# Two-layer streaming encoder on one core: both attentions reordered, a third slot for split weights, a third output chunk as filler, and the last chunk in token halves

## The chip, the cores and the metric

One core of a Trainium2 chip runs the whole kernel. The metric is device time in microseconds (us) of one execution; the kernel before has a median of 1163.75 us in 3 runs. TensorE (PE) multiplies, VectorE (DVE) and ScalarE (ACT) do the elementwise work, GpSimd (POOL) only constants and a few small powers, SyncE (SP) issues most transfers.

## The reference

The input is one sequence of 512 tokens of width 1024, all in f32. What is computed, cut down:

```python
# layer 0
h = rms_norm(x, norm_mix[0])
qa, ka, va, ra, ga, qb, kb, vb = split(h @ ab_w_in)        # GLA heads | stick-breaking heads
o_a = gla_chunk_causal(...); o_a = rms(o_a) * gla_norm * silu(ra)
o_b = stick_breaking(qb, kb, vb)                           # 8 heads of 64
x = x + concat([o_a, o_b]) @ ab_w_out
x = x + conv_ffn(rms_norm(x, norm_ffn[0]))
# layer 1
q, k, v = split(rms_norm(x, norm_mix[1]) @ c_w_qkv)        # 16 query heads, 4 key heads, window 128
x = x + swa_gqa_sinks(q, k, v, sinks, rel_bias) @ c_w_out
x = x + conv_ffn(rms_norm(x, norm_ffn[1]))
return rms_norm(x, norm_final)
```

Stick-breaking of one head needs z = q.k, then ln(1 + exp(-|z|)), a sum over later keys, an exp, and the product with v. The FFN is an up projection to 2 x 2816, a causal convolution of width 3, gelu(g) * val, and a down projection.

## The kernel before

The activations stand as features x tokens: `x` is 8 chunks of 128 features x 512 tokens. Every large product is made of three f32r matmuls (`three`, L1160 to L1162): an operand is split into a rounded high part and the rest, and hi.hi, hi.lo and lo.hi are summed in PSUM. So each weight unit of 128 x 1024 goes through these steps: a transfer into one of four `w_raw` buffers (SP), `hi` (ACT, L601, rounds it into `w_hi`), `lo` (DVE, L840, the rest into `w_lo`), then 24 matmuls of 512 columns. There are two slots of `w_hi`/`w_lo`, so unit u can be split only when unit u-2 is done.

Each engine runs its own program in order; semaphores join them. In the two mixers one list of steps, `SEQ0` and `SEQ1`, is built by hand and every engine walks it, taking its own part of each step. A weight unit is cut in eighths ("parts") so that attention steps can stand between them. The names in the lists:

- `("unit", u, (a, b))`: parts a to b of unit u on PE. When a unit ends, DVE evacuates it if it is a feature x token tile (L900, L903, L1080, L1083), and ACT if it belongs to a group that is token x feature (`vb`, `va`, `kg`, `v`; `b_evac`, L638, four tiles). Behind the unit stands `split`: `hi` and `lo` of a later unit.
- Layer 0, head h: `z` (PE L1311, L1314; ACT takes the absolute value), `z_exp` and `z_ln` (ACT L660, L663, 128 x 1280), `z_soft` (DVE: `sbS` L924, `sbH` L926, `sbL` L928), `sfx` (PE L1324 needs `sbL`; then ACT L667), `pv` (PE L1333, for two heads). `SB_PARTS` holds how many parts of filler stand between them.
- Layer 0, GLA: `gt`, `gz`, `gs`, `gd`, `gkv`, `go`, `gn`, `gout`, at places by `GLA_AT`, counted in parts. `gkv_v` (DVE L949, L952) makes the states that `go` (PE L1384) reads.
- Layer 1, head pair n: `s` (PE L1430; DVE L1111, L1121, L1124), `s_exp` (ACT L814, L817), `s_norm` (DVE, ends with L1134), `t` (PE transposes L1440, ACT copies L822), `o` (PE L1456; ACT L826, DVE L1139 split it). `v1s` is a copy of `v1` shifted by 64 tokens, made with two transfers issued by ACT (L802, L803) after the evacuation of `v`; every `o` needs it.
- `out`: blocks of an output chunk, which need the split attention output.

After a mixer come its eight output chunks (`w_out`, `out_tiles`), each added to `x` (L861), scaled and split into `h_hi` and `h_lo` (L612, L855) and squared into `ssq`. The 44 up units and 8 x 4 down units of the FFN follow in loops. At the end: the sum of squares over features (`ssq_mm`, L1206), variance (L873), power -0.5 on POOL (L588), a diagonal (L877), a broadcast matmul (`rinv_mm`, L1213), eight scalings of 128 x 512 (L1148) and eight output transfers (L545).

Of the kernel before, what the change touches and what calls it, by code (L numbers as in the profile page):

```python
# [27 lines left out]
F32 = mybir.dt.float32  # L28
# [33 lines left out]
MIX1 = [("k", 0), ("q", 0), ("q", 1), ("k", 1)] + [("q", i) for i in range(2, 7)] + [("v", 0), ("v", 1), ("q", 7)]  # L62
# [49 lines left out]
GLA_AT = ((42, "gt", 0), (45, "gz", 0), (49, "gz_v", 0), (56, "gs", 0), (60, "gd", 0), (62, "gd_v", 0),  # L112
# [120 lines left out]
def trunk(nc, xT, w_mix0, w_mix1, w_up, w_down, small, wg2, bias, out):  # L233
    ctx = ExitStack()
    with ctx:
# [79 lines left out]
        prTs = [s1(f"prT{n}", [P, NCH, P]) for n in range(CH // 2)]  # L315
# [8 lines left out]
        o1_lo = s1("o1_lo", [P, KC, T], F32R)  # L324
        m1.close()
# [268 lines left out]
        def _(act):  # L594
# [107 lines left out]
            def w_out(norm, u0, r0):  # L702

                for c in range(KC):
                    hi_static(u0 + c + SPL)
                    norm_tile(norm, c, r0 + c)

            def ffn(layer, norm, u_up, u_dn, r0, next_cols, last):
# [64 lines left out]

                def down_pair(i, final):

                    for kk in range(1, 9):
                        if not final or kk + SPL < 8:
# [3 lines left out]
                        if kk in (3, 7):  # L781
# [10 lines left out]
            for name, i, span in SEQ1:
                if name == "split":
                    hi_static(U_MIX1 + i + SPL)
                elif name == "unit" and span[1] == 8:
# [38 lines left out]
        def _(dve):  # L834
# [138 lines left out]
            def w_out(norm, u0, r0, units):  # L973
                for c in range(KC):
                    res_add(c, out_bank(c, units), u0 + c + 1)
                    lo_static(u0 + c + SPL)
                    res_split(norm, c, r0 + c)

            def ffn(layer, norm, u_up, u_dn, r0, next_cols, last):
# [74 lines left out]

                def down_pair(i, final):
                    for kk in range(1, 9):
                        j = kk // 4
                        if kk in (3, 7):
                            res_add(j + 2 * i, B_RES + j, u_dn + kk + 1 + 8 * i)
                        if not final or kk + SPL < 8:  # L1060
# [3 lines left out]
                        if kk in (3, 7):  # L1064
# [502 lines left out]
```

## Time and profile before

| | |
|---|---|
| median of 3 runs | 1163.75 us (1162.48 to 1165.25) |
| the profiled execution: its own time | 1162.42 us |
| its span, first to last instruction | 1160.7 us |
| PE busy | 1127.6 us, 97% |
| DVE, ACT busy | 653.8 us, 492.8 us |
| from the span's start to the last large matmul | 1145.07 us |

The rows of the profile name an engine, a line of the kernel and the tiles; "idle before" is the time in which the engine did nothing ahead of the instruction, with what ended it. The stages by the clock of the span: layer 0's mixer to about 235 us, its output and FFN to 640, layer 1's mixer to 755, its output and FFN to 1145, the final norm to the end.

### The profile page before, as it was taken

How to read it: one execution, taken by the hardware profiler on the slowest of the kernel's cores; microseconds unless marked ns; L12 is line 12 of the kernel's file. 1: busy time of each engine (PE TensorE's matmuls, PEld its weight loads, DVE VectorE, ACT ScalarE, POOL GpSimd, SP SyncE). 2: the span in 40 equal slices, each digit the busy share in tenths (PEclk: the TensorE clock that was granted, in tenths of full speed). 3: DMA queues.
4: the chain of work that ended last, by engine and by line, in shares of the span. 5: the costliest groups of instructions: out<-in, count | busy, mean ns of one | idle time of the engine just before them, and what ended most of it. 6: DMA issues, size and time to landing. Idle time of an engine off the chain costs nothing.

```text
span 1160.7 us, 15078 instructions
## 1 busy us (share of the span) xinstructions
PE 1127.6 (97%) x5402; PEld 918.6 (79%) x5402; DVE 653.8 (56%) x837; ACT 492.8 (42%) x714; POOL 8.6 (1%) x25
## 2 busy tenths in 40 slices
PE   8999999999999999999999999899999999999995
PEld 7776777778888888888888777688888888888884
DVE  6324343565777777774333565655777777763333
ACT  5547354843434434443332365634443443432220
POOL 1000000000000000000000000000000000000000
PEclk9999899999999999999999999999999999999997
DMA  5211111122232232223333222132222223233331
GB/s 225 73 55 55 55 55 55 55 91 91 91 107 92 90 106 93 90 77 94 94 99 120 98 73 89 38 104 89 98 90 103 95 90 106 77 85 93 97 86 72
DMA packets 31751, 102.92 MB, mean 89 GB/s; under 512 B 3537, under 2 KB 3682, under 8 KB 31714
## 3 DMA queue, kind: packets, MB, share of 16 engines
q1 hardware_dynamic: 30978, 100.17, 26.2%
q10 hardware_dynamic: 736, 2.24, 0.6%
q8 instruction: 25, 0.41, 0.1%
q14 instruction: 12, 0.10, 0.0%
HBM read 99.84 MB, written 2.10 MB: 88 GB/s over the span
## 4 chain that ended last, share of the span: by engine, by line
PE 59%; issue 32%; ACT 5%; DVE 4%; DMA 1%; POOLq 0%; POOL 0%; ACTq 0%; DVEq 0%; SPq 0%
PE ps L1160 17%; PE ps L1162 17%; PE ps L1161 17%; PE ps L1324 2%; PE ps L1311 2%; ACT pr L817 1%; ACT w_hi L601 1%; PE ps L1333 1%; DVE w_lo L840 1%; DMA x<-xT 1%; PE ps L1456 1%; DVE sc L1111 1%; ACT sbE L663 0%; DVE mx L1121 0%; DVE x L1148 0%
## 5 line engine op out<-in xcount | busy, mean ns | idle before, releaser
L601 ACT ACTIVATE w_hi<-w_raw 128x1024 fp32r<-128x1024 f32 (+1 forms) x203 | 198.1, 976 | 512.9 <-PE ps L1162 512.9
L840 DVE TENSOR_TENSOR w_lo<-w_raw,w_hi 128x1024 fp32r<-128x1024 f32 (+1 forms) x205 | 229.8, 1121 | 243.7 <-ACT w_hi L601 237.8
L1160 PE MATMUL ps<-h_hi,w_hi 128*128 128x512 f32 x896 | 355.6, 397 | 8.2 <-DVE h_lo L855 3.1
L1162 PE MATMUL ps<-h_hi,w_lo 128*128 128x512 f32 x896 | 349.6, 390 | 0.0
L1161 PE MATMUL ps<-h_lo,w_hi 128*128 128x512 f32 x896 | 349.6, 390 | 0.0
L1160 PEld LDWEIGHTS ps<-h_hi,w_hi 128*128 128x128 f32 x896 | 168.6, 188 | 48.1 <-issue 11.6
L1162 PEld LDWEIGHTS ps<-h_hi,w_lo 128*128 128x128 f32 x896 | 168.6, 188 | 35.4
L1161 PEld LDWEIGHTS ps<-h_lo,w_hi 128*128 128x128 f32 x896 | 168.7, 188 | 35.0 <-issue 1.2
L1160 PE MATMUL ps<-y_hi,w_hi 128*128 128x512 f32 x352 | 136.9, 389 | 0.0
L1161 PE MATMUL ps<-y_lo,w_hi 128*128 128x512 f32 x352 | 136.9, 389 | 0.0
L1162 PE MATMUL ps<-y_hi,w_lo 128*128 128x512 f32 x352 | 136.9, 389 | 0.0
L988 DVE TENSOR_TENSOR us<-ps,rinv 128x512 f32<-128x512 f32 x88 | 60.7, 692 | 84.7 <-PE ps L1162 84.7
L1160 PEld LDWEIGHTS ps<-y_hi,w_hi 128*128 128x128 f32 x352 | 66.1, 188 | 13.8
L1162 PEld LDWEIGHTS ps<-y_hi,w_lo 128*128 128x128 f32 x352 | 66.1, 188 | 13.8
L1161 PEld LDWEIGHTS ps<-y_lo,w_hi 128*128 128x128 f32 x352 | 66.1, 188 | 13.5
L998 DVE SCALAR_TENSOR_TENSOR cv<-us,par,cv 128x512 f32<-128x512 f32 x88 | 66.2, 752 | 11.0 <-DVE cv L995 0.6
L725 ACT ACTIVATE cv<-us,par 128x512 f32<-128x512 f32 x88 | 70.6, 804 | 2.9 <-DVE us L988 2.9
L995 DVE SCALAR_TENSOR_TENSOR cv<-us,par,cv 128x512 f32<-128x512 f32 x88 | 65.6, 746 | 0.6 <-ACT cv L725 0.6
L861 DVE TENSOR_TENSOR x<-ps,x 128x512 f32<-128x512 f32 (+1 forms) x32 | 22.1, 691 | 56.2 <-PE ps L1162 56.2
L1160 PE MATMUL ps<-w_hi,h_hi 128*128 128x512 f32 (+2 forms) x128 | 45.3, 354 | 2.7 <-DVE kbT L900 2.6
L1162 PE MATMUL ps<-w_hi,h_lo 128*128 128x512 f32 (+2 forms) x128 | 43.8, 342 | 0.0
L1161 PE MATMUL ps<-w_lo,h_hi 128*128 128x512 f32 (+2 forms) x128 | 43.8, 342 | 0.0
(181 smaller groups left out, 1050.6 us busy)
## 6 DMA issues: line engine op xcount, KB each, us to landing
w_raw<-w_up SPq DMA_DIRECT2D x88, 512.0 KB, 3.2
w_raw<-w_mix SPq DMA_DIRECT2D x53, 512.0 KB, 3.3
w_raw<-w_down SPq DMA_DIRECT2D x32, 384.0 KB, 3.1
w_raw<-w_down SPq DMA_DIRECT2D x32, 320.0 KB, 2.9
out<-x SPq DMA_DIRECT2D x8, 256.0 KB, 2.2
x<-xT SPq DMA_DIRECT2D x2, 512.0 KB, 8.0
x<-xT ACTq DMA_DIRECT2D x2, 512.0 KB, 8.7
bias_sb<-bias ACTq DMA_DIRECT2D x1, 512.0 KB, 3.9
```

The lines of the kernel that those rows point to most:

```text
L601: s.activation(w_hi[r % SPL][:, 0:cols], w_raw[r][:, 0:cols], ACT.Copy).then_inc(w_hi_ready, 1)
L725: s.activation(cv[k % 4][:, :], us[k % 2][:, 2:2 + T], ACT.Identity, bias=par[:, bass.ds(taps + 3, 1)], scale=par[:, bass.ds(taps + 2, 1)] ...
L840: v.tensor_tensor(w_lo[r % SPL][:, 0:cols], w_raw[r][:, 0:cols], w_hi[r % SPL][:, 0:cols].bitcast(F32), ALU.subtract).then_inc(w_lo_ready, 1)
L861: v.tensor_tensor(blk(x, c), ps[:, bank, :], blk(x, c), ALU.add).then_inc(x_updated, 1)
L988: v.tensor_tensor(us[k % 2][:, 2:2 + T], ps[:, k, :], rinv[:, :], ALU.mult).then_inc(u_scaled, 1)
L995: v.scalar_tensor_tensor(cv[k % 4][:, :], us[k % 2][:, 1:1 + T], par[:, bass.ds(taps + 1, 1)], cv[k % 4][:, :], ALU.mult, ALU.add).then_in ...
L998: v.scalar_tensor_tensor(cv[k % 4][:, :], us[k % 2][:, 0:T], par[:, bass.ds(taps, 1)], cv[k % 4][:, :], ALU.mult, ALU.add).then_inc(conv2, 1)
L1160: mm(dst, w[0], m[0], start=first, stop=False, skip_group_check=shared)
L1161: mm(dst, w[0], m[1], start=False, stop=False, skip_group_check=shared)
L1162: return mm(dst, w[1], m[0], start=False, stop=last, skip_group_check=shared)
L1311: mm(zs[:, ZOFF[b]:ZOFF[b] + ZW[b]], kbT[rows, j, b * P:(b + 1) * P], qbT[rows, j, b * P:T], start=b != 3, stop=False, skip_group_check=True)
L1324: ins = mm(dst, lhs[:, :], part[:, ZOFF[c]:ZOFF[c] + ZW[c]], start=False, stop=c == TT - 1 and part is sbL, skip_group_check=True)
```

## The change

1. `b_evac`: the last unit of a group `vb`, `va`, `kg` takes token tiles 1 and 0 first, then 3 and 2; a new semaphore `b_half` lets ACT evacuate two tiles in the middle of the unit and two at its end.
2. `SB_PARTS` and `GLA_AT` get other numbers. From `sfx` of head 1 on, the steps of the heads stand two parts of filler later. The order around the places that matter is listed below.
3. Layer 1: a third slot of `w_hi`/`w_lo` (in memory freed by sharing two of eight `prT` tiles), and each `split` works three units ahead in place of two, through the output chunks too. One more unit is split at the end of layer 0's FFN.
4. Layer 1: the two `v` units come before q6 and q7; `o` 0 to 5 stand earlier; a third output chunk (`out` 2) joins the two that fill PE between the last attention steps.
5. End: the weights of the last output chunk of the last down projection are split into the then free `h_hi`/`h_lo`, all 22 blocks, and used twice, for tokens 0 to 255 and then 256 to 511. The norm of a half, its scalings (128 x 256) and its transfers (256 KB, two chunks each, 1 KB runs) are done by halves; the sum and the broadcast of half 0 stand inside the matmuls of half 1 (before its blocks 5 and 14).

The order of the steps, cut to where it differs (kg1[2:4] is parts 2 and 3 of unit kg1):

```
layer 0, before: z_exp.1 kb1[3:5] z_ln.1 kb1[5:7] z_soft.1 kb1[7:8] split.7 kg0[0:7] sfx.1 kg0[7:8] split.8 kg1[0:2] z.2 pv.0 ...
layer 0, after:  z_exp.1 kb1[3:5] z_ln.1 kb1[5:8] split.7 z_soft.1 kg0 split.8 kg1[0:1] sfx.1 kg1[1:4] z.2 pv.0 ...
before: kg2[0:1] z_ln.2 kg2[1:3] z_soft.2 kg2[3:8] split.10 qb2[0:2] gt qb2[2:3] sfx.2 qb2[3:5] gz qb2[5:8]
after:  kg2[0:3] z_ln.2 kg2[3:5] z_soft.2 kg2[5:8] split.10 qb2[0:2] gt qb2[2:5] gz sfx.2 qb2[5:8]
before: z_exp.3 z_ln.3 kb2[5:7] z_soft.3 kb2[7:8] split.12 gs qb3[0:4] gd qb3[4:6] gd_v qb3[6:7] sfx.3
after:  z_exp.3 kb2[7:8] split.12 gs qb3[0:1] z_ln.3 qb3[1:3] z_soft.3 qb3[3:5] gd qb3[5:7] gd_v qb3[7:8] split.13 va0[0:1] sfx.3
before: z.6 pv.2 qa0[1:6] z_exp.6 z_ln.6 qa0[6:8] split.19 gkv.1 qa1[0:1] z_soft.6 qa1[1:4] gkv_v.1 qa1[4:8] split.20 ra0[0:2] sfx.6 ra0[2:3] go.0
after:  z.6 pv.2 qa0[3:8] split.19 gkv.1 z_exp.6 z_ln.6 qa1[0:3] z_soft.6 qa1[3:4] gkv_v.1 qa1[4:8] split.20 ra0[0:3] go.0 ra0[3:4] sfx.6
before: z_exp.7 ra1[2:3] go.1 go_v.1 ra1[3:4] z_ln.7 ra1[4:6] gn.0 z_soft.7 ra1[6:8] split.22 ra2[0:1] silu.0 ra2[1:3] gn_v.0 ra2[3:4] gn.1 ra2[4:6] sfx.7
after:  go.1 go_v.1 ra1[3:4] z_exp.7 ra1[4:6] gn.0 z_ln.7 ra1[6:8] split.22 z_soft.7 ra2[0:1] silu.0 ra2[1:3] gn_v.0 ra2[3:4] gn.1 ra2[4:8] split.23 sfx.7
layer 1, before: s.5 v0[5:7] t.4 v0[7:8] s_exp.5 v1[0:4] split.9 v1[4:6] s_norm.5 v1[6:8] q7[0:2] t.5 q7[2:4] split.10 o.0 o.1 q7[4:8]
  split.11 o.2 s.6 o.3 s_exp.6 s.7 out0[0,1] out1[0,1] s_norm.6 o.4 o.5 s_exp.7 out0[2,3] t.6 out0[4,5] s_norm.7 o.6 t.7 out1[2,3] o.7 ...
layer 1, after:  s.5 v1[5:7] t.4 v1[7:8] s_exp.5 q6[0:4] split.9 q6[4:6] s_norm.5 q6[6:8] q7[0:2] t.5 o.0 q7[2:4] split.10 o.1 o.2 q7[4:8]
  split.11 o.3 s.6 o.4 o.5 s.7 s_exp.6 out0[0..5] s_norm.6 s_exp.7 out1[0..3] t.6 out1[4,5] s_norm.7 o.6 out2[0,1] t.7 out2[2,3] o.7 ...
```

The diff, cut to its core:

```diff
-SB_PARTS = ((4,), (5, 2, 2, 2, 8), (3, 2, 5, 2, 8), (8, 2, 0, 2, 8), (5, 2, 2, 3, 8), (2, 1, 1, 7, 8),
-            (3, 5, 0, 3, 9), (5, 3, 2, 2, 8), (9,))
+SB_PARTS = ((4,), (5, 2, 2, 3, 9), (3, 2, 5, 2, 8), (8, 2, 2, 2, 6), (5, 2, 2, 3, 8), (2, 1, 1, 7, 8),
+            (3, 5, 0, 3, 9), (5, 3, 2, 2, 8), (7,))
-... (60, "gd", 0), (62, "gd_v", 0),
+... (61, "gd", 0), (63, "gd_v", 0),
+SPL1 = 3
+def slot(u):
+    return (U_MIX1 % 2, (U_MIX1 + 1) % 2, 2)[(u - U_MIX1) % 3] if U_MIX1 <= u < U_UP1 else u % SPL
+def slot_free(u):
+    last = [k for k in range(u) if slot(k) == slot(u)]
+    return max(last[-1] + 1 if last else 0, U_UP0 if slot(u) >= SPL else 0)
+        def out_bank(c, units):
+            if units is MIX1 and c in (2, 3):
+                return B_SC + c - 2
...
+                        if span[0] < 4 <= span[1]:
+                            act.wait_ge(b_half, b_before(MIX0, i + 1) // TT)
+                            b_evac(dst, B_COLS[n], b_tile, order[0:2])
+                        if span[1] == 8:
+                            act.wait_ge(unit_done, i + 1)
+                            b_evac(dst, B_COLS[n], b_tile, order[2:4])
...
-                    hi_static(U_MIX1 + i + SPL)
+                    hi_static(U_MIX1 + i + SPL1)
...
             def w_out(norm, u0, r0, ahead):
                 for c in range(KC):
-                    hi_static(u0 + c + SPL)
+                    if c + ahead < KC + SPL:
+                        hi_static(u0 + c + ahead)
                     norm_tile(norm, c, r0 + c)
...
+            def down_tail(u_dn, r0):
+                ...
+                for half in range(2):
+                    toks = tok_half(half)
+                    for k in range(4):
+                        if half == 0:
+                            pe.wait_ge(w_lo_ready, u_dn + 4 * (KC - 1) + k + 1)
+                        for b in range(DN[k]):
+                            c = DOFF[k] + b
+                            if half == 1 and c == SSQ_AT:
+                                last_sum(0)
+                            if half == 1 and c == RBC_AT:
+                                last_rbc(0)
+                            w = tuple(last_w(t, k)[:, b * P:(b + 1) * P] for t in (h_hi, h_lo))
+                            ins = three(ps[:, B_LAST[half], 0:TH], w, (y_hi[:, c, toks], y_lo[:, c, toks]),
+                                        c == 0, c == FC - 1)
+                    ins.then_inc(half_done, 1)
+                last_sum(1)
+                last_rbc(1)
```

On DVE the end now runs, per half: add, (for half 1: scaling 5 of half 0), `ssq` add, variance, (for half 1: scalings 6 and 7 of half 0), diagonal, then scalings 0 to 4 of half 0 or 0 to 7 of half 1.

## Rows read from the trace of the kernel before

**Rows 1.** Windows: length, busy time of PE, PEld, DVE, ACT, POOL (instructions), then granted clock, DMA, GB/s.

```profile
34.00:235.00 201.00, 192.10 (x1037) 148.94 (x1036) 83.82 (x92) 112.72 (x107) 0.00 (x0) 0.97 0.17 56
660.00:755.00 95.00, 87.80 (x619) 71.50 (x618) 59.18 (x83) 55.66 (x179) 0.00 (x0) 1.00 0.20 67
```

**Rows 2.** Waits of PE in the two mixers: total, times, longest.

```profile
PE ps L1160 <- DVE kbT L900: 2.6, 1, 2.6
PE ps L1360 <- ACT gE L680: 1.8, 1, 1.8
...
PE ps L1160 <- DVE w_lo L840: 3.2, 3, 1.2
PE ps L1456 <- DMA v1s<-v: 1.6, 1, 1.6
```

**Rows 3.** Windows around three waits of PE.

```profile
67.26:69.87 2.61, 0.00 (x0) 0.00 (x0) 2.58 (x4) 0.30 (x1) 0.00 (x0) 0.91 0.00 0
69.87:72.76 2.89, 2.89 (x13) 2.89 (x13) 1.08 (x1) 0.00 (x0) 0.00 (x0) 0.50 0.25 61
...
116.97:120.26 3.29, 3.29 (x16) 3.29 (x17) 3.29 (x4) 0.00 (x0) 0.00 (x0) 0.53 0.00 0
120.26:124.13 3.87, 3.87 (x10) 3.06 (x11) 0.16 (x1) 0.18 (x1) 0.00 (x0) 0.52 0.41 135
718.90:720.50 1.60, 0.00 (x0) 0.02 (x1) 0.96 (x1) 0.61 (x1) 0.00 (x0) 1.00 0.16 51
```

**Rows 4.** ACT in time order, 179 to 184: start, length, instruction.

```profile
179.84 1.28 ACT L663 ACT_TABLE_LOAD   x1
181.13 1.28 ACT L663 ACTIVATE sbE<-sbE 128x1280 f32<-128x1280 f32 x1
183.09 1.06 ACT L601 ACTIVATE w_hi<-w_raw 128x1024 fp32r<-128x1024 f32 x1 [0.68 <-PE ps L1162]
```

**Rows 5.** DVE in time order, 185 to 192.

```profile
185.32 1.48 DVE L924 SCALAR_TENSOR_TENSOR sbS<-ps,sbE 128x1280 f32<-128x1280 f32 x1
...
189.11 0.28 DVE L949 COPY kbT<-ps 128x128 f32<-128x128 f32 x1
189.43 2.65 DVE L952 SCALAR_TENSOR_TENSOR kbT<-kbT,dec,ps 128x128 f32<-128x128 f32 x7
```

**Rows 6.** ACT in time order, layer 1, 709 to 717.

```profile
709.01 0.49 ACT L814 ACTIVATE es<-nm,par 128x4 f32<-128x4 f32 x2 [0.30 <-DVE nm L1124]
712.48 1.05 ACT L601 ACTIVATE w_hi<-w_raw 128x1024 fp32r<-128x1024 f32 x1
714.15 1.57 ACT L638 ACTIVATE v<-ps,rinv_col 128x256 f32<-128x256 f32 x4 [0.62 <-PE ps L1162]
715.75 0.52 ACTq L802 DMA_DIRECT2D v1s<-v  x1
716.30 0.61 ACTq L803 DMA_DIRECT2D v1s<-v  x1
```

**Rows 7.** PE's transposes `t.5`.

```profile
716.41 1.09 PE L1440 MATMUL ps<-ident,pr 128*128 128x128 f32 x8
```

**Rows 8.** DVE as the output chunks end, 784 to 788.

```profile
784.16 0.69 DVE L861 TENSOR_TENSOR x<-ps,x 128x512 f32<-128x512 f32 x1 [1.85 <-PE ps L1162]
785.31 1.23 DVE L840 TENSOR_TENSOR w_lo<-w_raw,w_hi 128x1024 fp32r<-128x1024 f32 x1 [0.46 <-ACT w_hi L601]
786.45 0.75 DVE L855 SCALAR_TENSOR_TENSOR h_lo<-x,par,h_hi 128x512 fp32r<-128x512 f32 x1
```

**Rows 9.** Windows of steady matmuls: 256 columns, 512 columns.

```profile
707.40:713.70 6.30, 6.30 (x55) 6.30 (x54) 1.64 (x4) 5.55 (x20) 0.00 (x0) 1.00 0.03 12
1120.00:1140.00 20.00, 20.00 (x90) 16.57 (x89) 6.51 (x8) 4.44 (x7) 0.00 (x0) 1.00 0.12 33
```

**Rows 10.** The end in time order.

```profile
1150.52 2.08 PE L1213 MATMUL ps<-sq,ones 128*128 128x512 f32 x2 [2.07 <-DVE sq L877]
1152.63 5.36 DVE L1148 SCALAR_TENSOR_TENSOR x<-x,par,ps 128x512 f32<-128x512 f32 x8 [2.17 <-PE ps L1213]
```

More of the change, by code:

```diff
@@ L61 @@
 N0 = len(MIX0)
-MIX1 = [("k", 0), ("q", 0), ("q", 1), ("k", 1)] + [("q", i) for i in range(2, 7)] + [("v", 0), ("v", 1), ("q", 7)]
+MIX1 = [("k", 0), ("q", 0), ("q", 1), ("k", 1)] + [("q", i) for i in range(2, 6)] + [("v", 0), ("v", 1), ("q", 6), ("q", 7)]
 N1 = len(MIX1)
@@ L314, in trunk @@
         prs = [s1(f"pr{k}", [P, NCH, P]) for k in range(2)]
-        prTs = [s1(f"prT{n}", [P, NCH, P]) for n in range(CH // 2)]
+        prTs = [s1(f"prT{n}", [P, NCH, P]) for n in range(CH // 2 - 2)]
+        prTs += prTs[0:2]
         mx = s1("mx", [P, NCH])
@@ L434, in trunk @@
         warmed = sem("warmed")
+        half_done = sem("half_done")
         out_ready = sem("out_ready")
@@ L772, in ffn, with last_hi, last_squares @@
                     later_stages(UP // 4 - 1, k)
+                def last_hi(k):
+                    u = u_dn + 4 * (KC - 1) + k
+                    act.wait_ge(w_loaded[u % RAW], 16 * (u // RAW) + 16)
+                    act.wait_ge(unit_done, u_dn)
+                    s.activation(last_w(h_hi, k), w_raw[u % RAW][:, 0:DN[k] * P], ACT.Copy).then_inc(w_hi_ready, 1)
+                def last_squares():
+                    for half in range(2):
+                        act.wait_ge(x_updated, r0 + KC + half)
+                        act.wait_ge(ssq_added, (norm + 1) * NADD + KC)
+                        s.activation(sq[:, tok_half(half)], x[:, KC - 1, tok_half(half)],
+                                     ACT.Square).then_inc(sq_ready, 1)
                 def down_pair(i, final):
                     for kk in range(1, 9):
-                        if not final or kk + SPL < 8:
+                        if last and final and 4 <= kk + SPL < 8:
+                            last_hi(kk + SPL - 4)
+                        elif not final or kk + SPL < 8:
                             down_hi(i, kk, DN[(kk + SPL) % 4] * P)
@@ L1057, in down_pair @@
                         j = kk // 4
-                        if kk in (3, 7):
+                        tail = last and final and kk == 7
+                        if kk in (3, 7) and not tail:
                             res_add(j + 2 * i, B_RES + j, u_dn + kk + 1 + 8 * i)
-                        if not final or kk + SPL < 8:
+                        if last and final and 4 <= kk + SPL < 8:
+                            last_lo(kk + SPL - 4)
+                        elif not final or kk + SPL < 8:
                             down_lo(i, kk, DN[(kk + SPL) % 4] * P)
@@ L1063, in down_pair @@
                             down_lo(i, kk, next_cols[kk + SPL - 8])
-                        if kk in (3, 7):
+                        if kk in (3, 7) and not tail:
                             res_split(norm + 1, j + 2 * i, r0 + j + 2 * i, last)
@@ L1180, in b_unit @@
             def b_unit(u, part, parts, tile, n_cols, span=(0, 8), a_taken_by=None):
+                low_first = tile is b_tile and part == parts - 1
                 if span[0] == 0:
@@ L1193, in b_unit @@
                     tok = slice(tt * P, (tt + 1) * P)
-                    ins = three(tile(tt, n_cols), (h_hi[:, c, tok], h_lo[:, c, tok]), w_blocks(u % RAW, k, n_cols),
+                    ins = three(tile(tt, n_cols), (h_hi[:, c, tok], h_lo[:, c, tok]), w_blocks(slot(u), k, n_cols),
                                 c == 0 and (tile is b_tile or tt % 2 == 1), c == KC - 1, tile is v_tile)
+                    if low_first and step == steps // 2 - 1:
+                        ins.then_inc(b_half, 1)
                 if span[1] == 8:
```

189 lines of the change are left out of this document (130 added, 59 removed).

## The prediction

> **What bounds the kernel now.** The page comes first: PE is busy for 1127.6 of 1160.7 us, so only its idle time and its slow matmuls can be won. The windows by stage place the idle time: layer 0's mixer has 201.0 - 192.1 = 8.9 us, layer 1's 95.0 - 87.8 = 7.2 [rows 1]; the start (some 5) is not touched, the FFN loops have none, and 15.6 us follow the last large matmul (1145.07 to 1160.7). The waits of PE name causes: 2.6 for kbT, which DVE evacuates behind `z_soft.1`; 1.8 for ACT's exp ahead of `gd`; 3.2 in three waits for `lo`; 1.6 for the v1s transfer [rows 2]. Windows around them show a second price: the granted clock fell to 0.50, the 1.2 GHz level, late in the 2.6 us wait, and the 12 matmuls behind took 2.89 us; it fell again behind the 1.8 us wait, where `gd` took 3.29 and nine matmuls 3.87. Behind the 1.6 us wait it stayed at 1.00 [rows 3]. At full clock a matmul takes 0.227 us for 512 columns (20.0 us, 88 whole ones) and 0.122 for 256 (52 in 6.3) [rows 9]; a part of a unit is three of 512, 0.68.
>
> The sums are made against the span of 1160.7. The profiled execution's own time was 1162.4, 1.3 under the median of the runs, and I carry the difference over.
>
> **Layer 0, what goes.** Half-group evacuation ends the wait behind vb3 (0.8). With `z_soft.1` behind kb1's evacuation the 2.6 go; with `gs` ahead of `z_ln.3` the 1.8. The rest is short. I take off all 8.9 and add below what I find. The slow stretches go too: 12 matmuls of 272 columns at 0.127 would be 1.5, which gives 1.4; nine of 512 give 1.8; `gd`, all of it at 0.53, gives between 0 and 1.65, and I take 1.4, near the ratio of clocks. Together 4.6.
>
> **Layer 0, what comes.** I walked the programs of ACT and DVE in the new order with these durations. kb1 ends at 64.0, ACT does `hi` until 65.4, DVE `lo` until 66.7 and `z_soft.1` (3.8, from 185.32 to 189.11 [rows 5]) until 70.6. PE is at `sfx.1` at 69.0: wait 1.65. qb2 still waits for the first kg tile, now behind `z_ln.2` in ACT: 1.1. `gz` now precedes `sfx.2` and finds DVE in `z_soft.2`: 1.3. Around va and `gkv.0`: 1.4 in three pieces. Two waits are long.
>
> - `go.0`. `z_exp.6` now stands behind `split.19`, whose `hi` needs the end of qa0. Before, exp and ln ran inside qa0 and `hi` came behind them, at 183.09 [rows 4]. Now, from the end of qa0: hi, exp, table load, ln 4.9 [rows 4], `z_soft.6` 3.8, `gkv_v.1` 2.9 (189.11 to 192.08 [rows 5]), the evacuation of qa1 0.7 [rows 8]: 12.3. PE arrives after `gkv.1` (about 1.5), qa1 and three parts: 9.0. Wait 3.3. `sfx.6`, which stood in this gap, is queued behind it.
> - `sfx.7`. From the end of `go.1`: a copy, exp, load, ln of `gn.0`, load, exp, load, `z_ln.7`, `hi`. That is three loads and two 128x1280 passes at 1.28 and four 128x1024 passes at 1.06 [rows 4, 6], 10.7; then `lo` 1.2 [rows 8] and `z_soft.7` 3.8: 15.7. PE has 13 parts and two `gn`, 8.8 + 3.4 (a `gn` is two products like the 2.08 us one of half clock [rows 10], at full clock): 12.2. Wait 3.5.
>
> Out1 waits 0.5 for its weights. New idle time: 12.75. At the long two I expect the clock to fall, as in the wait of 2.6. The price of a fall lies between 1.4 and 3.5 (the two seen); dense matmuls follow here too, so I take 1.4 each, 2.8. Layer 0: -8.9 - 4.6 + 12.75 + 2.8 = +2.1.
>
> In the row a load takes 1.28 us and the next ACTIVATE starts 1.29 after it [rows 4]. The Trainium skill ("ScalarE: Activation LUTs", What ACT_TABLE_LOAD costs) adds a drain of about 1.38 us to each switch; by it the wait at `sfx.7` would be some 4 us longer. Its section on table sets names a set with both exp and ln; by it the three loads would go and the wait would be nil. The trace has loads between exp and ln, and no drain behind them; it agrees with neither.
>
> **Layer 1.** With three slots the splits are a unit ahead: the three waits for `lo` (3.2) go. `v` earlier ends the 1.6 for v1s; the longer filler ends those for the bias add and the copy of prT (1.2 each). I take off 7.2, and 0.6 for restarts saved (0.16 each over the idle row, four fewer). What comes:
>
> - `t.5`. v1 now ends ahead of `s_exp.5`, and ACT evacuates it and issues both v1s transfers there: 714.15 to 716.9 before, 2.75 [rows 6]. PE runs 1.3 earlier here, so v1 ends at 706.8, the copy of `t.4` at 707.3, and `s_exp.5` starts at 710.0. From there to `t.5` it took 716.41 - 709.01 = 7.4 [rows 6, 7]: 717.4. PE arrives at 713.6. Wait 3.8; queued behind it are the `o` steps. The transfers themselves are long done.
> - `s.7` waits 0.3 for DVE's add.
> - At the end of the output chunks, `hi` and `lo` of the second up unit take a two-slot buffer again, so they need the end of chunk 7, and they stand ahead of chunk 6's norm step. h_lo of chunk 7 was there 3.0 after the chunk's end (784.16 to 787.2 [rows 8]); now `lo`, chunk 6's two steps and chunk 7's add precede it: 5.8. PE needs it at 4.8. Wait 1.1.
> - A fall of the clock in the 3.8 us: 1.4.
>
> The extra split at the start stands behind all that the first norm needs; SP's loads start earlier, never later. Layer 1: -7.8 + 3.8 + 0.3 + 1.1 + 1.4 = -1.2.
>
> **The end.** 132 matmuls of 256 columns in place of 66 of 512: 16.1 - 15.0 = +1.1. The sum and broadcast of half 0 inside half 1: +1.0. Behind the last matmul: add, square and sum at 256 columns save 0.27 each (the slope of DVE), the diagonal 0.27, the sum's matmuls 0.5, the broadcast 0.9 of 2.08, eight scalings 8 x (0.67 - 0.40) = 2.2 of 5.36 [rows 10]: -4.7. Half 0's scalings fit in half 1 and in POOL's time. The last transfer is again 256 KB; 1 KB runs cost between 0 and 0.7 (if its rate halved), and I take 0, since one is issued per 0.8 us and not per 0.67. The last weights' splits have the same size and lie under chunk 6. End: -2.6.
>
> Sum: +2.1 - 1.2 - 2.6 = -1.7: span 1159.0, median **1162.0**.
>
> **Rivals.**
> - *The long waits aren't there.* For: the steps sit only two parts later, and the old order had no such wait there. Against: each follows from an order of one engine's program. Price: `go.0` 3.3, `sfx.7` 3.5, `t.5` 3.8 and their three falls 4.2. All gone: 1147.2. One gone: about 1157. Chance 0.35, of it 0.08 for all.
> - *The clock stays low (slower).* One mechanism: behind each long wait the clock stays at 0.5 as long as from 117 to 124, 3.5 us of price in place of 1.4 [rows 3]; with `go.0`, `sfx.7`, `t.5` that is 6.3 more: 1168.3. It decides for slower from 2.9 per fall. For: tiny or transpose matmuls follow two of the waits, as `gd` did. Against: the fall in the 2.6 us wait cost 1.4. Chance 0.17. The Trainium skill ("TensorE: Matmul & The Clock Gate", Why this matters for your kernels) warns against idle gaps between bursts because they cost the full rate, which speaks against a change that makes three gaps longer than any now inside the kernel.
> - *Half-size matmuls are bound by their weight loads.* A load is busy for 0.186 (16.57 us over 89 [rows 9]); at that pace the end costs 24.6 - 16.1 = 8.5 more: 1170.5. The row of 256 columns speaks against it [rows 9]. Chance 0.03.
> - *The end gives nothing* (restarts, the transfers): 1164.6. Chance 0.07.
>
> My forecast: 0.38. A measurement of this kernel can't tell under 0.2%, 2.3 us, from no change. Around 1162.0 a third of the forecast's chance lies under 1161.4: faster 0.35 + 0.12, same 0.26 + 0.08 for the last rival and the mild part of the second, slower the rest. The range takes in one long wait less, with something over, and three dear falls: 1155 to 1168. The forecast's own is 1159 to 1165.
>
> **What would show it.** Right: no PE wait for kbT or `gd`; waits over 3 us at L1384, L1324 near 215 and L1440 near 715, each with the clock at 0.5 behind it; no `lo` wait in layer 1 but one for h_lo at the first up unit; the last matmul some 13 us before the end. Wrong: PE busy throughout both mixers, or a clock of 1.00 behind the long waits; a tail over 14 us; 256 column matmuls at over 0.13.

## The result: the change makes the kernel 0.2% slower

The changed kernel takes 1167.0 us (median of 18 runs, 1160.5 to 1169.0), the kernel before 1163.7 (18 runs, 1162.3 to 1165.3). The ratio is 1.0021, 95% interval 1.0011 to 1.0030. The forecast was 1162.0 in a range of 1155 to 1168, with most of the chance on faster or unchanged: the measured time lies in that wide range, but on the other side of the kernel before. One thing is visible before any profile: the runs of the new kernel are spread over 8.5 us, those of the old one over 3.

The profiled execution took 1168.5 us. The head of its page:

```profile
span 1166.8 us, 15220 instructions
PE 1136.3 (97%) x5470; PEld 930.7 (80%) x5470; DVE 654.2 (56%) x849; ACT 493.9 (42%) x716; POOL 9.0 (1%) x26
```

Windows of layer 0's mixer, of layer 1's (8 us later here), and of the last output chunk and the tail behind it, columns as in [rows 1]:

```profile
34.00:235.00 201.00, 189.93 (x1005) 148.99 (x1003) 80.26 (x87) 110.02 (x104) 0.00 (x0) 0.95 0.16 56
668.00:772.00 104.00, 98.96 (x659) 81.61 (x658) 62.57 (x88) 59.00 (x183) 0.00 (x0) 0.97 0.20 67
...
1139.30:1155.90 16.60, 16.60 (x139) 16.54 (x137) 7.11 (x14) 2.31 (x4) 0.70 (x1) 1.00 0.05 15
1155.90:1166.80 10.90, 2.08 (x9) 1.07 (x7) 5.82 (x15) 0.42 (x1) 0.70 (x1) 0.66 0.51 171
```

Layer 0 now has 11.1 us of idle time, against 8.9 in [rows 1]; its mean clock is 0.95 against 0.97. Layer 1 has 5.0 against 7.2 (6.2 with the wait of 1.2 at the first up unit, which is at 798, behind the window), but its clock is 0.97 where it was 1.00. The last chunk and the tail take 27.5 us; before it was 15.0 + 15.8 = 30.8:

```profile
1129.90:1144.90 15.00, 15.00 (x67) 12.22 (x66) 3.90 (x5) 2.85 (x4) 0.00 (x0) 1.00 0.00 1
1144.90:1160.70 15.80, 3.45 (x11) 1.62 (x10) 7.60 (x12) 0.63 (x1) 1.01 (x1) 0.60 0.36 133
```

The waits of PE, as in [rows 2]:

```profile
PE ps L1477 <- DVE sbL L999: 5.0, 2, 3.5
PE ps L1264 <- DVE h_lo L926: 3.8, 2, 2.6
PE ps L1593 <- DVE pr L1217: 3.7, 1, 3.7
PE ps L1537 <- DVE qaT L974: 3.1, 1, 3.1
...
PE ps L1499 <- DVE gaT L1006: 1.2, 1, 1.2
PE ps L1583 <- DVE q L1166: 0.9, 1, 0.9
```

The waits for kbT, gE, `lo` and v1s are gone. In their place stand `sfx.7` (3.5) and `sfx.1` (1.5) on L1477, `t.5` (3.7), `go.0` (3.1), `gz` (1.2) and the wait at the first up unit (1.2 of the 3.8 for h_lo; the 2.6 are at the start). What follows four of them is in windows of 10 us:

```profile
92.00:102.00 10.00, 8.85 (x33) 7.59 (x34) 1.00 (x2) 6.23 (x6) 0.00 (x0) 0.66 0.16 54
189.00:199.00 10.00, 8.63 (x56) 8.03 (x57) 2.41 (x4) 2.33 (x3) 0.00 (x0) 0.66 0.15 54
223.00:233.00 10.00, 8.39 (x32) 7.61 (x33) 6.99 (x9) 6.86 (x8) 0.00 (x0) 0.66 0.21 74
724.00:734.00 10.00, 7.46 (x48) 5.97 (x50) 4.94 (x7) 2.57 (x3) 0.00 (x0) 0.66 0.15 52
```

These are `gz`, `go.0`, `sfx.7` and `t.5`. The clock has only the levels 0.50 and 1.00 here, so a mean of 0.66 over 10 us is 6.8 us at 1.2 GHz: 10 x (1 - 0.66) = 3.4 us of full-clock time lost, four times. Such a stretch is called a fall below. What falls into the wait itself costs nothing: behind `gz` the fall begins after the wait and costs all of its 3.4; the other three begin 0.4 to 0.7 us before their wait ends and cost 3.1 to 3.2 each, 12.9 for the four. The kernel before, read the same way around its two falls [rows 3], lost 1.7 and 3.4:

```profile
68.00:78.00 10.00, 8.13 (x48) 7.70 (x49) 2.97 (x4) 2.26 (x2) 0.00 (x0) 0.83 0.16 53
116.00:126.00 10.00, 9.03 (x38) 8.12 (x39) 4.38 (x5) 1.11 (x2) 0.00 (x0) 0.66 0.16 52
```

### The profile page after: what moved, and what is told of

Read it like the earlier page. It is cut to its first block, busy times and chain, and to the rows that moved or that the text cites. A ratio compares the mean times of both kernels' runs of the same rounds, so it can differ in the third digit from the quotient of the medians.

```text
span 1166.8 us, 15220 instructions
## 1 busy us (share of the span) xinstructions
PE 1136.3 (97%) x5470; PEld 930.7 (80%) x5470; DVE 654.2 (56%) x849; ACT 493.9 (42%) x716; POOL 9.0 (1%) x26
## 4 chain that ended last, share of the span: by engine, by line
PE 88%; ACT 5%; DVE 4%; issue 2%; DMA 1%; ACTq 0%; POOLq 0%; POOL 0%; DVEq 0%; SPq 0%
PE ps L1264 27%; PE ps L1265 26%; PE ps L1266 26%; PE ps L1477 2%; PE ps L1464 2%; ACT pr L885 2%; ACT w_hi L647 1%; PE ps L1486 1%; PE ps L1609 1%; DVE w_lo L914 1%; ACT L710 1%; DMA x<-xT 1%; DVE sbS L995 1%; PE ps L1593 0%; PE ps L1537 0%
## 5 line engine op out<-in xcount | busy, mean ns | idle before, releaser
L640 ACT ACTIVATE w_hi<-w_raw 128x1024 fp32r<-128x1024 f32 (+2 forms) x146 | 139.0, 952 | 418.6 <-PE ps L1266 418.6
L908 DVE TENSOR_TENSOR w_lo<-w_raw,w_hi 128x1024 fp32r<-128x1024 f32 (+2 forms) x146 | 158.9, 1089 | 151.8 <-ACT w_hi L640 151.0
L1264 PE MATMUL ps<-y_hi,w_hi 128*128 128x512 f32 x330 | 128.4, 389 | 0.0
L1265 PE MATMUL ps<-y_lo,w_hi 128*128 128x512 f32 x330 | 128.4, 389 | 0.0
L1266 PE MATMUL ps<-y_hi,w_lo 128*128 128x512 f32 x330 | 128.4, 389 | 0.0
L914 DVE TENSOR_TENSOR w_lo<-w_raw,w_hi 128x1024 fp32r<-128x1024 f32 x55 | 67.3, 1223 | 81.5 <-ACT w_hi L647 76.2
L647 ACT ACTIVATE w_hi<-w_raw 128x1024 fp32r<-128x1024 f32 x53 | 55.9, 1055 | 84.9 <-PE ps L1266 84.9
L1264 PEld LDWEIGHTS ps<-y_hi,w_hi 128*128 128x128 f32 x330 | 61.9, 188 | 12.9
L1266 PEld LDWEIGHTS ps<-y_hi,w_lo 128*128 128x128 f32 x330 | 61.9, 188 | 12.8
L1265 PEld LDWEIGHTS ps<-y_lo,w_hi 128*128 128x128 f32 x330 | 61.9, 188 | 12.8
```

Of the source, the lines that this page charges most:

```text
L640: s.activation(w_hi[r % SPL][:, 0:cols], w_raw[r][:, 0:cols], ACT.Copy).then_inc(w_hi_ready, 1)
L647: s.activation(w_hi[n][:, :], w_raw[r][:, :], ACT.Copy).then_inc(w_hi_ready, 1)
L908: v.tensor_tensor(w_lo[r % SPL][:, 0:cols], w_raw[r][:, 0:cols], w_hi[r % SPL][:, 0:cols].bitcast(F32), ALU.subtract).then_inc(w_lo_ready, 1)
L914: v.tensor_tensor(w_lo[slot(u)][:, :], w_raw[u % RAW][:, :], w_hi[slot(u)][:, :].bitcast(F32), ALU.subtract).then_inc(w_lo_ready, 1)
L1264: mm(dst, w[0], m[0], start=first, stop=False, skip_group_check=shared)
L1265: mm(dst, w[0], m[1], start=False, stop=False, skip_group_check=shared)
```

## The experiments

"Filled" below means matmuls that nobody reads, put in front of a wait in TensorE's program. The other edits take parts of the change back or move steps. Every time is a median beside the kernel before on the same chip (1163.6 to 1163.8 in every set).

**The end alone (end_only).** Both mixers as before (but for the order in which TensorE takes the token tiles of the last unit of a group); only the end is the changed one. Against the changed kernel, besides the old tables and the old `mix1_order`:

```diff
-SPL1 = 3
+SPL1 = 2
...
-    return (U_MIX1 % 2, (U_MIX1 + 1) % 2, 2)[(u - U_MIX1) % 3] if U_MIX1 <= u < U_UP1 else u % SPL
+    return u % SPL
...
-                        if span[0] < 4 <= span[1]:
+                        if False:
...
-                            b_evac(dst, B_COLS[n], b_tile, order[2:4])
+                            b_evac(dst, B_COLS[n], b_tile, order)
```

> The kernel before with nothing of the change but the end in token halves (both attentions in the old order, two slots, whole-group evictions). My theory: the end gives 2.6 us as forecast (4.7 less behind the last matmul, 2.1 more for half matmuls and for the sum and broadcast of half 0), so about 1161.1 against 1163.7, ratio 0.998. Rival, the end gives nothing: 1163.7. Rival, half-size matmuls are bound by their loads: 1172. If it gives more than 2.6, then the two attentions lose more than the 5 to 6 us that I now put down to them.

Measured: 1158.9, ratio 0.9966 (0.9954 to 0.9979). The end gives 4.7, more than forecast. Its profile has

```profile
1128.40:1145.10 16.70, 16.70 (x139) 16.59 (x138) 7.11 (x14) 2.31 (x4) 0.69 (x1) 1.00 0.05 16
1145.10:1155.40 10.30, 1.50 (x8) 0.82 (x6) 5.82 (x15) 0.42 (x1) 0.69 (x1) 0.76 0.54 179
```

27.0 us in place of 30.8: the last chunk costs 1.7 more (forecast 2.1) and the tail 5.5 less (forecast 4.7). So 3.8 are seen there; the other 0.9 is within what the intervals leave open. Part of it may be the clock: this profiled execution (1157.1) waits 2.6 us for kbT in the old order, as before, but has no fall there:

```profile
68.00:78.00 10.00, 8.30 (x54) 7.30 (x55) 4.00 (x4) 2.26 (x2) 0.00 (x0) 1.00 0.16 55
```

**Layer 0 and the end (l0_and_end).** The changed kernel with layer 1 as before: of the edits above those of `SPL1`, `slot` and `mix1_order`.

> The changed kernel with layer 1 as before (order, two slots, two output chunks); layer 0's new order, half-group evictions and the end stay. In the trace of the changed kernel layer 0 has idle time 11.1 against 8.9 us and three stretches of half clock that cost 3.4 each against two of 1.7 and 3.4: about +7.3 us for layer 0. With the end at -2.6: 1163.7 + 7.3 - 2.6 = 1168.4, waits of 3.1 at the product with qaT and 3.5 at the last suffix product, each with half clock behind it. Rival, most of the loss is in layer 1: under 1165.

Measured: 1165.5, 1.0015 (1.0004 to 1.0026), runs from 1160.5 to 1168.5. The waits came back at 3.08 and 3.55, but the stretches behind them are half as long:

```profile
188.00:198.00 10.00, 8.97 (x64) 8.13 (x65) 2.08 (x3) 3.55 (x3) 0.00 (x0) 0.83 0.16 54
220.00:230.00 10.00, 8.13 (x37) 7.30 (x38) 7.36 (x9) 7.12 (x8) 0.00 (x0) 0.83 0.26 89
```

The same 32 matmuls of `go.0`, behind the same wait, in this kernel:

```profile
189.03 2.00 PE L1530 MATMUL ps<-qaT,qbT 64*128 64x64 f32 x32 [3.08 <-DVE qaT L968]
```

and in the changed kernel:

```profile
190.37 3.68 PE L1537 MATMUL ps<-qaT,qbT 64*128 64x64 f32 x32 [3.09 <-DVE qaT L974]
```

Nothing that comes before them differs between the two kernels. So a fall behind one and the same wait costs 1.7 or 3.4, and the order of the work doesn't say which. The profiles differ in when the fall begins: 2.3 us after the wait's end here, 0.4 us before it in the changed kernel.

```profile
190.00:191.00 1.00, 1.00 (x21) 0.93 (x17) 0.11 (x1) 0.00 (x0) 0.00 (x0) 1.00 0.00 0
191.00:192.00 1.00, 1.00 (x5) 0.86 (x4) 0.00 (x0) 0.92 (x1) 0.00 (x0) 0.64 0.69 184
```

The same moment in the changed kernel, whose wait ends at 190.37:

```profile
189.00:190.00 1.00, 0.00 (x0) 0.00 (x0) 0.96 (x3) 0.00 (x0) 0.00 (x0) 1.00 0.00 0
190.00:191.00 1.00, 0.63 (x6) 0.63 (x8) 1.00 (x2) 0.00 (x0) 0.00 (x0) 0.50 0.00 0
```

The mixers have twelve waits of over 3 us in all profiles together, each with a fall. The eight falls that began before their wait had ended cost 3.4, the four that began after it 1.7. For shorter waits this doesn't hold (the 2.6 for kbT: 0.5 before its end, 1.7; the 1.8 for `gd`: 0.2 after, 3.4). What sets the moment of the fall no run shows.

**Layer 0's order as before (l0_old).**

```diff
-SB_PARTS = ((4,), (5, 2, 2, 3, 9), (3, 2, 5, 2, 8), (8, 2, 2, 2, 6), ..., (7,))
+SB_PARTS = ((4,), (5, 2, 2, 2, 8), (3, 2, 5, 2, 8), (8, 2, 0, 2, 8), ..., (9,))
```

(and `gd` one part earlier, as before).

> The changed kernel with layer 0's order tables of the kernel before (half-group evictions, layer 1 and the end stay changed). Against the kernel with the end alone (1158.9) it has layer 1's change and the half-group evictions: 7.2 us of idle time and 0.6 of restarts less, waits of 3.7, 0.95, 1.2 and 0.2 more, and 1.7 to 3.4 of clock behind the 3.7: 1157 to 1160, likeliest 1158.5. Layer 0's new order then costs the rest up to 1167, some 8.5. Rival, layer 1 is where the loss is: over 1162.

Measured: 1158.3, 0.9958 (0.9946 to 0.9971), runs within 1.0 us. Against the end alone, layer 1's change and the half-group evictions come to 0.7 together, which the intervals don't tell from nothing. Layer 0's new order costs 1167.0 - 1158.3 = 8.8, or 7.9 against the second set of the changed kernel (1166.1, below), which ran on the same chip. That is where the loss is.

**The waits filled (fill4).** This separates what a wait costs by its length from what the clock costs behind it.

```diff
+            def fill(n, bank):
+                for _ in range(n):
+                    mm(ps[:, bank, :], h_hi[:, 0, 0:P], h_hi[:, 0, :], start=True, stop=True)
...
                 elif name == "go":
+                    if i == 0:
+                        pe.wait_ge(oc_lo_ready, 3)
+                        fill(13, B_O)
```

> The changed kernel, and in its program of TensorE extra matmuls that are read by nobody (h_hi by h_hi, 512 columns, into a bank that is free then) ahead of four waits: 5 ahead of gz, 13 ahead of go.0, 15 ahead of sfx.7, 15 ahead of t.5, at 0.227 each 1.1, 3.0, 3.4 and 3.4 us, so as long as the waits of 1.16, 3.09, 3.54 and 3.67. No other engine's order changes, the time to each wait's end stays, only that TensorE works through it. My theory: a wait costs its own length and besides 3.4 us of half clock behind it, and the fall comes from the idle time: the four falls go, 4 x 3.4 = 13.6 less than the profiled 1168.5: about 1155. With a price of 1.4 for each fall, as I had forecast: 1163 or so. If falls come for another reason than the idle time (the tiny matmuls themselves), 1167, no change.

Measured: 1158.1, 0.9946 (0.9933 to 0.9959): 9.0 less than the changed kernel, with all its orders and all its waiting. In the profile layer 0 is at a clock of 1.00 throughout:

```profile
34.00:235.00 201.00, 196.95 (x1077) 152.52 (x1076) 84.09 (x92) 114.87 (x109) 0.00 (x0) 1.00 0.17 56
```

Four falls at 3.4 would have been 13.6. The filling itself costs 1.0 to 1.6. The 1.6 is by the runs of both kernels (span times mean clock): 1149.9 against 1148.3. The 1.0 is by the two profiles: from the end of the wait at `sfx.1` to the end of the one at the first up unit it is 714.9 us here, and 726.8 less the falls' 12.9 = 713.9 in the changed kernel. That leaves (9.0 + 1.0) / 4 = 2.5 to (9.0 + 1.6) / 4 = 2.7 us of clock for a wait on average, between 1.7 and 3.4.

**Half filled (half_fill).**

```diff
-                        fill(13, B_O)
+                        fill(6, B_O)
```

and 8 in place of 15 ahead of `sfx.7` and of `t.5`.

> The changed kernel with extra matmuls that nobody reads ahead of the same four waits as in the kernel that filled them, but for about half of the three long ones: 6 ahead of go.0, 8 ahead of sfx.7 and 8 ahead of t.5 (1.4 and twice 1.8 us), 5 ahead of gz as there. Idle gaps of 1.7 to 1.9 are left where there were 3.1 to 3.7. If a gap's length decides whether the clock falls, so that under 2 us it mostly doesn't: about 1158, like the filled one. If a gap of 1.8 is as good as one of 3.6 for a fall (as the 1.8 us in front of gd was in the kernel before): three falls of 1.7 to 3.4, 1163 to 1167. Likeliest, some of both: 1161, with a wide spread.

Measured: 1157.7, 0.9957 (0.9942 to 0.9971), but spread from 1155.3 to 1161.5. Idle gaps of 1.7 to 1.8 were left; in the profile one of the three was followed by a fall, of 1.7, behind `go.0`. So gaps of this size bring a fall now and then; gaps over 3 us inside the mixers did in every profile. At the very start, where the clock rose to 1.00 only 2 us or so before the wait, it is otherwise: waits of 3.1 (the kernel before), 3.2 (this one) and 3.4 (`l0_old`) for the first h_lo had no fall. The likeliest value I had written down, 1161, was too high.

**The old kernel filled (before_fill).**

```diff
+                    if a_taken_by is not None and c == 0 and tt == 1 and u == 8:
+                        pe.wait_ge(rinv_ready, 1)
+                        fill(11, B_O)
...
                 elif name == "gd":
+                    pe.wait_ge(oc_lo_ready, 1)
+                    fill(8, B_O)
```

> The kernel before, its orders unchanged, with 11 such matmuls ahead of the wait of 2.6 us for kbT and 8 ahead of the wait of 1.8 for gd, which fill them. The two falls in its profile cost 1.7 and 3.4. If the idle time is what brings the falls: 5.1 less, 1158.6. If the 16 tiny matmuls of gd (128x2) bring the second fall and not the wait: 1.7 less, 1162.

Measured: 1159.0, 0.9966 (0.9955 to 0.9978), 4.6 less. Around `gd` the clock is now 1.00:

```profile
112.00:124.00 12.00, 11.98 (x69) 10.23 (x69) 7.37 (x7) 5.21 (x7) 0.00 (x0) 1.00 0.13 45
```

The idle time brought the falls, not the 16 tiny matmuls behind it.

**The changed kernel again (again).**

> The changed kernel once more, nothing different, for a second profile. The waits are set by the orders of the programs and should come back within 0.1 us: 3.1 at go.0, 3.5 at sfx.7, 3.7 at t.5, 1.2 at gz. My theory is now that what a wait costs beside its length varies from one execution to the next: 3.4 us of clock behind it in the first profile, 1.7 behind the same waits in the kernel with layer 1 as before. So some of the four stretches are 3.4 and some 1.7 or absent, and the runs spread from 1160 to 1169 again, with the span less the lost clock the same for all (1148.1 in the first). Rival, the cost of a fall is fixed and the spread has another source: all four at 3.4 again.

Measured: 1166.1, 1.0013 (1.0001 to 1.0025). The waits came back within 0.1, but so did the four stretches at 3.4 each: by this profile the price looks fixed, as the rival had it. Its runs speak for the spread (time, mean clock, span times clock):

```
1162.8  0.989  1148.2        1166.7  0.985  1147.4
1163.2  0.989  1148.7        1167.7  0.985  1148.3
1166.1  0.987  1149.3        1168.7  0.984  1148.1
```

These are six of the eleven runs; the others have 1147.4 to 1148.5 in the last column, which the rounding of the clock leaves open by some 0.6. That column stays within 2 while the time moves by 5.9: the spread is the clock's, in one and the same program, and the profiled executions were among the dear ones (1168.5 and 1167.7).

**Heads 6 and 7 back (heads67).** The two long waits of layer 0 are removed by their order.

```diff
-            (3, 5, 0, 3, 9), (5, 3, 2, 2, 8), (7,))
+            (1, 5, 0, 3, 9), (5, 3, 2, 2, 8), (9,))
```

> The changed kernel, with the steps of heads 6 and 7 in layer 0 at the places of the kernel before (z.6 at part 1 of qa0, exp and ln of head 6 inside qa0 and so ahead of its split; sfx.6 ahead of go.0); the rest as changed. My theory: the waits of 3.1 at go.0 and 3.5 at sfx.7 go and with them two falls of the clock at 3.4: 13.4 less than the profiled 1168.5, about 1155. If only the waits count and the falls move elsewhere: 1161. If other waits take their place (the chain of DVE is the same length either way): 1165 or more.

Measured: 1154.8, 0.9929 (0.9916 to 0.9941): 12.3 less than the changed kernel.

```profile
34.00:235.00 201.00, 195.38 (x1072) 151.77 (x1071) 88.92 (x98) 116.83 (x113) 0.00 (x0) 1.00 0.18 58
```

Idle time in layer 0 went from 11.1 to 5.6, and all falls are gone, the one behind `gz` too, though that wait is still 1.2. A new one, of 1.7, stands at 782 behind the 1.2 us wait for h_lo. Short waits bring falls in some executions and not in others. The unchanged wait at `gz` shows it: a fall of 3.4 in both profiles of the changed kernel, of 1.7 in `l0_and_end` and `heads67_t5` (below), none here. A wait of 1.2 for the first kg tile stands 5 us ahead of it, with no fall right behind it in any profile; where only `gz`'s wait is filled or gone there is none in that place.

**v1 evacuated later (heads67_t5).** The lines with v1 are moved, from ScalarE's part of `unit` to that of `split`.

```diff
                 if name == "split":
                     hi_static(U_MIX1 + i + SPL1)
+                    if MIX1[i] == ("v", 1):
+                        act.wait_ge(unit_done, U_MIX1 + i + 1)
+                        b_evac(v1, CKV * CD, v_tile, b_order(0))
+                        act.wait_ge(b_taken, B_MIX0 + TT)
+                        act.dma_start(v1s[0:CHUNK, 1:TT, :], v1[CHUNK:P, 0:TT - 1, :]).then_inc(vs_loaded[0], 16)
+                        act.dma_start(v1s[CHUNK:P, :, :], v1[0:CHUNK, :, :]).then_inc(vs_loaded[1], 16)
```

> The kernel with heads 6 and 7 in their old places (1154.8) and besides, in ScalarE's program, the evacuation of v1 and the two v1s transfers moved from ahead of exp.5 to behind the split that follows it. exp.5 then starts when its row maxima are there, 2.4 us sooner; o.0 needs v1s only behind t.5. My theory: the wait of 3.7 at t.5 falls to 1.3 and the fall behind it is shorter or gone: 2.4 + 1.7 less, about 1150.5. Rival, v1s is now late and o.0 waits for the transfer instead: 1153 to 1155.

Measured: 1157.1, 0.9939 (0.9926 to 0.9953): the rival, and a little worse than it. `t.5` did fall to 1.3, but `o.0` now waits for v1s:

```profile
711.80 1.09 PE L1593 MATMUL ps<-ident,pr 128*128 128x128 f32 x8 [1.31 <-DVE pr L1217]
716.81 0.69 PE L1609 MATMUL ps<-prT,v1s 128*64 128x128 f32 x4 [3.92 <-DMA v1s<-v]
```

**All mended (all_mended).** Besides: `gz` behind `sfx.2`, and the split of the second up unit behind chunk 7's norm step.

```diff
-(45, "gz", 0)
+(47, "gz", 0)
...
-                    if c + ahead < KC + SPL:
+                    if c + ahead < KC + 1:
                         hi_static(u0 + c + ahead)
                     norm_tile(norm, c, r0 + c)
+                hi_static(u0 + KC + 1)
```

> All mendings at once: heads 6 and 7 in their old places, v1's evacuation behind exp.5, the split of the second up unit behind chunk 7's norm step (takes the wait of 1.2 for h_lo, and its fall where there is one), gz two parts later, behind sfx.2 as in the kernel before (takes the wait of 1.2 and its fall of 1.7 to 3.4). My theory: 1150.5 - 1.2 - 1.2 - 2.5 = about 1145.5, and a spread of under 3 us, since no long wait is left inside. Rival, short waits of 1.3 to 1.5 (sfx.1, t.5) go on costing falls at random: about 1148.

Measured: 1152.8, 0.9906 (0.9891 to 0.9920). The waits at `gz` and for h_lo behind layer 1's output chunks are gone. v1s is as late as in the kernel before this one (3.9 again, with 3.4 of clock behind it); I had left that out of the expectation, which was made before it was known.

**The norm first (norm_first), and v1s from GpSimd (v1s_gpsimd).** v1's evacuation is back ahead of exp.5.

```diff
+SEQ1.remove(("split", 9, None))
+SEQ1.insert(SEQ1.index(("s_norm", 5, None)) + 1, ("split", 9, None))
```

and for the second kernel, in GpSimd's program, with ScalarE's two transfers taken out:

```diff
+                if norm == 2:
+                    pool.wait_ge(b_taken, B_MIX0 + TT)
+                    g.dma_start(v1s[0:CHUNK, 1:TT, :], v1[CHUNK:P, 0:TT - 1, :]).then_inc(vs_loaded[0], 16)
+                    g.dma_start(v1s[CHUNK:P, :, :], v1[0:CHUNK, :, :]).then_inc(vs_loaded[1], 16)
```

> The kernel with all mendings (1152.8), but v1's evacuation and transfers back where the changed kernel has them (ahead of exp.5), and instead head pair 5's normalization ahead of the split of unit 9, whose weights nobody needs before the output chunks. The split's hi and lo (1.04 and 1.23 us) then leave the chain to t.5: its wait goes from 3.7 to about 1.5, and o.0 doesn't wait for v1s, which was issued 4 us earlier. My theory: against the 1.3 + 3.9 of the kernel with all mendings 3.7 less and a fall of 1.7 to 3.4 less where it doesn't fall at 1.5: 1147. Rival, the fall stays at the wait of 1.5: 1149 to 1150.

> The same, and the two v1s transfers are issued by GpSimd, which is idle there, so that exp.5 starts 1.1 us sooner. My theory: the wait at t.5 is 0.3 to 0.5, no fall: 1145.5 to 1147. Rival, issuing from GpSimd makes the transfers later than o.0 needs them, as they were 3.9 us late when ScalarE issued them behind the split: 1150.

Measured: 1146.3, 0.9854 (0.9839 to 0.9869), and 1144.8, 0.9841 (0.9828 to 0.9855). In the first `t.5` waits 1.6 and the clock stays at 1.00; in the second it doesn't wait at all, and the two transfers of v1s land 2.8 and 3.2 us after their issue:

```profile
640.00:760.00 120.00, 118.50 (x765) 97.20 (x764) 74.17 (x102) 66.31 (x192) 1.23 (x2) 1.00 0.23 76
```

This version is 18.9 us under the kernel before and 22.3 under the changed one, with every part of the change kept but the places of a few steps.

## Why the prediction was wrong

**The waits were right, one by one.** Gone as said: kbT, `gd`, the three for `lo`, v1s. Come as said (forecast, measured): `sfx.1` 1.65, 1.47; the kg tile 1.1, 1.2; `gz` 1.3, 1.16; `go.0` 3.3, 3.09; `sfx.7` 3.5, 3.54; `t.5` 3.8, 3.67; h_lo 1.1, 1.18; out1 0.5, 0.41 (which the kernel before has too). The 0.3 at `s.7` didn't come; a wait of 0.23 stands one step earlier, at `o.5`. Too high was the 1.4 around va and `gkv.0`: 0.6. Not foreseen: 0.95 for q at one of the first score steps of layer 1, which I didn't trace further. The walk of `sfx.7` holds three table loads of 1.28 and no drain between a load and the pass behind it, as for `z_ln.7`:

```profile
216.00 1.28 ACT L710 ACT_TABLE_LOAD   x1
217.29 1.27 ACT L710 ACTIVATE sbE<-sbE 128x1280 f32<-128x1280 f32 x1
```

By the drain that the Trainium skill names ("ScalarE: Activation LUTs", What ACT_TABLE_LOAD costs) the wait would have been about 4 longer; the measurement decides against it here.

**The step that failed** is a size: "The price of a fall lies between 1.4 and 3.5 (the two seen); dense matmuls follow here too, so I take 1.4 each". In both profiles of the changed kernel each of the three lost 3.4, of it 3.1 to 3.3 while TensorE worked: 9.5 in place of 4.2 (over its runs the average is 2.5 to 2.7 a fall). The 1.4 itself was well read: the fall behind kbT lost 1.7 in all, of which 0.25 lay in the wait. The error was to carry it over to three other waits. The kernel before had another fall that cost 3.4, and I chose between the two by the kind of matmul that follows, which doesn't decide it: `go.0` lost 1.7 in one kernel and 3.4 in the other with identical work, and dense matmuls follow `sfx.7`, which lost 3.4. The middle of the two prices, 2.5 each, would have added 3.2 to the sum.

**A term was missing:** a fall behind `gz`. I gave none to waits under 2 us, although [rows 3] had one behind a wait of 1.8. It cost 3.4 in both profiles of this kernel, 1.7 in two others and nothing in `heads67`. The first profile has one more at the start, 1.7 at 9 to 13 us, the second has none. The steps up to there are the same in all kernels. Still, of the ten profiles with layer 0's new order seven have a fall there (1.7 or 3.4), of the four with the old order none; whether that is chance stays open.

**The sum, again.** Forecast -1.7 on the span, profiled +6.1. Of the 7.8 between them the falls are 12.9 - 4.2 = 8.7, the start 0.8 (1.5 of a fall, and 0.7 less of waiting) and layer 1's waits 0.8 (6.0 in place of 5.2: the 0.95 for q, and small differences); against that stand 1.3 less idle time in layer 0 (11.5 in place of 12.75), 0.7 more from the end and 0.3 more from the two falls that went (4.9 in place of 4.6). These come to 8.0, 0.2 more than the 7.8. The 0.6 for restarts was not looked for. On medians, with falls at 2.5 to 2.7 on average, four are 10.0 to 10.8, 5.8 to 6.6 above what I had counted; that covers the 5.0 by which the median was missed. By parts: end -4.7 (forecast -2.6), layer 1 with the half evictions -0.7 (forecast about -2; with layer 0's new order in front, layer 1's change comes out at +1.5, 1167.0 against 1165.5, so its sign stays open), layer 0's order +7.9 to +8.8 (forecast +2.1 with those evictions). One sign that I had named can't have come from my own sum: "the last matmul some 13 us before the end". The 15.6 of before less the 4.7 behind the last matmul are 10.9, and 10.9 it is (1155.9 to 1166.8); 13 takes off the 2.6 of the whole end. The half evictions were not tried by themselves; the 0.8 for vb3 is gone from the changed kernel's waits, as forecast.

**The rivals.** "The clock stays low" is the mechanism that the profiles of the changed kernel show, and it deserved more than 0.17. That its time is met (1168.3 against 1168.5 profiled) is in part luck: it had three falls at 3.5, there were four at 3.2 on average and other misses that offset each other; the median is 1167.0, and in `l0_and_end` the clock came back after half as long. Its turning point for slower, given as 2.9 per fall, is 2.8 by the numbers beside it. Its argument "for", tiny matmuls behind the wait, was as void as mine "against". The warning of the Trainium skill ("TensorE: Matmul & The Clock Gate", Why this matters for your kernels) against idle gaps between bursts agrees with the filled kernels, 9.0 and 4.6 us. The other rivals are refuted: the long waits are there, half-size matmuls run at 0.120, and the end gives more than forecast.

## What to carry to other kernels

Price a wait of TensorE as its length plus the clock behind it, and take that second price as a spread (here 1.7 or 3.4 us, 2.5 to 2.7 on average, behind each gap over 3 us inside the mixers and sometimes behind one of 1.2) and not as the one value seen last; many short waits in place of a few long ones is no gain if some of the new ones are long. When a step of ScalarE or VectorE is moved behind a split, walk its chain to the next wait: two parts later can be 3 us and a fall. Fill a disputed wait with matmuls that nobody reads: the time that comes back, and the little that the filling costs (here 1.0 to 1.6 for 48 matmuls), is the clock's share; what is left is the wait's.

## What the runs showed of the hardware that I had not expected

- A fall of the clock in or behind a wait loses 1.7 or 3.4 us wherever it comes before the final norm in the fourteen profiles, nothing between, and which one differs between executions with the same work in front. Behind waits of over 3 us inside the mixers it was 3.4 in the eight cases in which the clock fell before the wait's end, and 1.7 in the four in which it fell after it.
- Matmuls of 256 columns follow each other every 0.120 us (1144.77, 1144.89, 1145.01 in the kernel with the end alone), so halving the token width costs little: 16.7 for the chunk in place of 15.0.
- The same two v1s transfers (448 KB) took 2.7 to 3.2 us from issue to landing in the changed kernel, 3.7 to 4.1 before, and 5.3 to 5.7 in the kernel that issued them later. There 6.4 us at 154 GB/s make 985 KB, which leaves room for one 512 KB weight transfer beside them. In the changed kernel 3.4 us at 135 GB/s make 459 KB, the transfers alone:

```profile
710.40:716.80 6.40, 1.18 (x9) 0.88 (x9) 1.91 (x3) 1.02 (x1) 0.00 (x0) 0.87 0.57 154
```

```profile
717.80:721.20 3.40, 3.40 (x17) 2.82 (x16) 0.00 (x0) 2.08 (x12) 0.00 (x0) 1.00 0.55 135
```
